# A hybrid attention and delta-rule layer on one core: masks behind the first level's sums, one more block of side work in the levels, and the attention merge behind the last level

## The reference, cut to what matters

```
kk = einsum('nbhid,nbhjd->nbhij', kc * bc, kc)
lower = where(tri_strict, kk * decay, 0) + eye(c)
sol = triangular_solve(lower, concat([vc * bc, kc * bc * exp(gcum)]))
attn = einsum('nbhid,nbhjd->nbhij', qc, kc) * decay
def step(s, xs):                     # one chunk after the other
    u = u0 - wk @ s
    o = qd @ s + attn @ u
    s = s * g_last + kd^T @ u
...
w = softmax(stack(lses), axis=0)     # merge of the three attention groups
o_att = sum(w[..., None] * stack(outs), axis=0)
```

## Time and profile before

| | |
|---|---|
| median of 3 runs | 1901.26 us (1900.22 to 1904.27) |
| the profiled execution | 1900.11 us, of it the span 1898.3 us |
| mean granted TensorE clock | 0.975 |
| TensorE busy in the span | 1793.2 us (94%) |
| VectorE, ScalarE, GpSimd busy | 45%, 28%, 21% |

### The profile page before, as it was taken

The page is one execution under the profiler, slowest core; times in us unless marked ns, Lnnn a source line. Parts: engine busy times, 40 slices in busy tenths (PEclk is TensorE's granted clock), DMA queues, the critical chain, the costliest instruction groups (busy, mean ns, idle before and its releaser), DMA issues.

```text
span 1898.3 us, 36967 instructions
## 1 busy us (share of the span) xinstructions
PE 1793.2 (94%) x14992; PEld 1735.9 (91%) x14992; DVE 845.2 (45%) x1548; ACT 533.9 (28%) x1048; POOL 393.4 (21%) x194
## 2 busy tenths in 40 slices
PE   7999999999978888999999779999999999999995
PEld 7999999999968787887999779999999999999994
DVE  3003346664545566645651444452144441144437
ACT  3223334444312333330221353331012221022211
POOL 2221111111111110111222342222222222222224
PEclk9999999999989999998999889999999999999997
DMA  4111112242522132314541113333333111111111
GB/s 169 44 44 43 42 64 76 80 179 82 214 86 90 61 108 72 97 46 169 200 160 45 45 67 116 128 120 117 116 117 127 44 44 45 45 47 53 41 62 78
DMA packets 68233, 170.13 MB, mean 90 GB/s; under 512 B 9448, under 2 KB 38280, under 8 KB 66832
## 3 DMA queue, kind: packets, MB, share of 16 engines
q1 hardware_dynamic: 67408, 167.68, 25.7%
q10 hardware_dynamic: 720, 0.92, 0.1%
HBM read 138.19 MB, written 57.79 MB: 103 GB/s over the span
## 4 chain that ended last, share of the span: by engine, by line
PE 85%; DVE 8%; issue 2%; DMA 2%; ACT 2%; POOL 1%; POOLq 0%; SPq 0%; DVEq 0%; ACTq 0%
PE U L720 60%; PE U L824 7%; PE U L1190 3%; PE B L720 2%; PE B L810 1%; PE B L785 1%; DMA stage<-in_wu 1%; PE B L802 1%; DVE stats L1973 1%; PE B L913 1%; PE B L987 1%; PE B L1138 1%; PE B L1015 1%; PE B L915 1%; DVE og L1683 1%
## 5 line engine op out<-in xcount | busy, mean ns | idle before, releaser
L638 POOL TENSOR_TENSOR wl<-stage,wh 128x1024 fp32r<-128x1024 f32 x127 | 310.3, 2444 | 1127.6 <-ACT wh L1211 1127.6
L720 PE MATMUL U<-xh,wh 128*128 128x344 f32 x1368 | 443.6, 324 | 0.2 <-ACT qkv L1215 0.2
L720 PE MATMUL U<-xl,wh 128*128 128x344 f32 x1368 | 437.1, 320 | 0.0
L720 PE MATMUL U<-xh,wl 128*128 128x344 f32 x1368 | 437.1, 319 | 0.0
L720 PE MATMUL U<-hh,wh 128*128 128x344 f32 x1056 | 338.8, 321 | 4.5 <-POOL hl L691 4.5
L720 PE MATMUL U<-hl,wh 128*128 128x344 f32 x1056 | 338.2, 320 | 0.0
L720 PE MATMUL U<-hh,wl 128*128 128x344 f32 x1056 | 337.4, 319 | 0.0
L720 PEld LDWEIGHTS U<-xh,wh 128*128 128x128 f32 x1368 | 257.3, 188 | 0.8 <-ACT qkv L1215 0.5
L720 PEld LDWEIGHTS U<-xh,wl 128*128 128x128 f32 x1368 | 257.2, 188 | 0.0
L720 PEld LDWEIGHTS U<-xl,wh 128*128 128x128 f32 x1368 | 257.1, 188 | 0.0
L720 PEld LDWEIGHTS U<-hh,wh 128*128 128x128 f32 x1056 | 199.3, 189 | 4.6 <-issue 4.6
(11 more groups left out here) (359 smaller groups left out, 2468.3 us busy)
## 6 DMA issues: line engine op xcount, KB each, us to landing
stage<-in_wu SPq DMA_DIRECT2D x126, 512.0 KB, 3.6
out_shift<-in_cache SPq DMA_DIRECT2D x16, 1022.0 KB
gate_scr<-gth SPq DMA_DIRECT2D x16, 516.0 KB, 3.0
gates<-gate_scr SPq DMA_DIRECT2D x8, 1032.0 KB, 5.0
dn_scr<-thb SPq DMA_DIRECT2D x12, 512.0 KB, 2.6
qkv<-in_xT SPq DMA_DIRECT2D x4, 1032.0 KB, 10.5
kvc<-in_cache SPq DMA_DIRECT2D x4, 1024.0 KB, 8.4
dqk<-dn_scr SPq DMA_DIRECT2D x8, 512.0 KB, 3.9
```

The source lines that it names most:

```text
L638: nc.gpsimd.tensor_tensor(wl[:, par, :], stage[:, par, :], wh[:, par, :].bitcast(F32), ALU.subtract).then_inc(w_lo, 1)
L720: ins = nc.tensor.matmul(dst, a[:, par, w], b[:, xk, third(j)], start=first and n == 0 and m == 0, stop=last and n == len(ks) - 1 and m == 2)
```

## The change

Four moves, all inside the tile loop; no instruction is added or taken away.

1. `FILLS[1]`: the quarters of the six levels go from (1, 0, 1, 0, 0, 2) to (1, 1, 2, 1, 1, 2). What `beside.rest()` has left behind level 5 goes from 7 quarters to 3.
2. `masks` is cut: `Loff` and `ATm` go to `late_masks`, which VectorE runs behind both additions of level 0, with `out_low(i - 2)` and the `amx` maxima behind it. The level 1 quarter stands before `state_read`, which waits for `ATm`.
3. VectorE's merge of the attention groups goes from levels 2 and 3 behind `out_norms(i - 1)`.
4. TensorE's turn of `ao` goes from level 5 behind `beside.rest()`, and ScalarE's `oh` copy behind its own `rest()`.

```diff
-FILLS = {1: (0, 2, 4, 1, (1, 0, 1, 0, 0, 2), 2), ...
+FILLS = {1: (0, 2, 4, 1, (1, 1, 2, 1, 1, 2), 2), ...
@@ TensorE, inside `for lv in range(LEVELS)`, behind y
                     if i > 0 and lv in (1, 3, 4):
+                        if lv == 1:
+                            beside.run(f_level[lv])
                         (state_read, updates, outputs)[lv // 2 if lv < 4 else 2](i - 1)
                     if lv == 5:
-                        pe.wait_ge(ao_ready, i + 1)
-                        pe.wait_ge(s_ready, i + 1)
-                        for n in range(2):
-                            ins = nc.tensor.transpose(B34[:, 0, n * P:(n + 1) * P], ao[:].rearrange(
-                                "p h e -> p (h e)")[:, n * P:(n + 1) * P], ident)
-                        ins.then_inc(ao_done, 1)
-                    beside.run(f_level[lv] + (2 if i == 0 and lv in (1, 3, 4) else 0))
+                        beside.run(f_level[lv])
+                    if lv not in (1, 5) or i == 0 and lv == 1:
+                        beside.run(f_level[lv] + (2 if i == 0 and lv in (1, 3, 4) else 0))
...
                 beside.rest()
+                pe.wait_ge(ao_ready, i + 1)
+                pe.wait_ge(s_ready, i + 1)
+                for n in range(2):
+                    ins = nc.tensor.transpose(B34[:, 0, n * P:(n + 1) * P], ...
+                ins.then_inc(ao_done, 1)
@@ VectorE, in masks
+            def late_masks(t):
                 nc.vector.scalar_tensor_tensor(Loff[LO], LT4[LO, :, HB:P], -1.0, Ew[LO, :, HB:P], ALU.mult, ALU.mult)
                 nc.vector.tensor_tensor(heads4(ATm[:, t % 2]), AT4, Ew[:], ALU.mult).then_inc(side_ready, 1)
@@ VectorE, behind the additions of level 0
                     if lv == 0:
+                        late_masks(i)
+                        if i > 1:
+                            out_low(i - 2)
+                        (the three amx maxima)
                         query_norms(i)
@@ VectorE, behind the levels
                     out_norms(i - 1)
+                dve.wait_ge(ae_exp, i + 1)
+                (abuf times weights, two additions, reciprocal, ao)
                 dve.wait_ge(ao_high, i + 2)
```

More of the change, by code:

```diff
@@ L402, in tiles @@
                 u += n
-        FILLS = {1: (0, 2, 4, 1, (1, 0, 1, 0, 0, 2), 2), 2: (2, 4, 6, 2, (2, 1, 2, 1, 1, 3), 4)}
+        FILLS = {1: (0, 2, 4, 1, (1, 1, 2, 1, 1, 2), 2), 2: (2, 4, 6, 2, (2, 1, 2, 1, 1, 3), 4)}
         def window(t):
@@ L1030, in _ @@
                 beside.rest()
+                pe.wait_ge(ao_ready, i + 1)
+                pe.wait_ge(s_ready, i + 1)
+                for n in range(2):
+                    ins = nc.tensor.transpose(B34[:, 0, n * P:(n + 1) * P], ao[:].rearrange(
+                        "p h e -> p (h e)")[:, n * P:(n + 1) * P], ident)
+                ins.then_inc(ao_done, 1)
             beside = Beside(U_BRANCH - BESIDE_SAMPLES, (U_BRANCH - BESIDE_SAMPLES) % 2, BESIDE_SAMPLES, quarter, start_unit)
@@ L1425, in _ @@
                     out_squares(i - 1)
+                beside.rest()
                 act.wait_ge(ao_done, i + 1)
@@ L1428, in _ @@
                     "p (n k) -> p n k", n=2), ACT.Copy).then_inc(ao_high, 1)
-                beside.rest()
             beside = Beside(U_BRANCH - BESIDE_SAMPLES, (U_BRANCH - BESIDE_SAMPLES) % 2, BESIDE_SAMPLES, quarter, start_unit)
@@ L1818, in _ @@
                 masks(i)
-                if i > 1:
-                    out_low(i - 2)
                 for lv in range(LEVELS):
@@ L1825, in _ @@
                         dn.link(nc.vector.tensor_tensor(Lb[lv % 2][:], LTq[:], lev(lv + 2), ALU.mult))
[L1827 to L1832, removed]
                     if lv < LEVELS - 1:
@@ L1852, in _ @@
                     if lv == 0:
+                        late_masks(i)
+                        if i > 1:
+                            out_low(i - 2)
+                        dve.wait_ge(att_in, i * 16 + 16)
+                        dn.link(nc.vector.tensor_tensor(amx[:, 0, :], abuf[:, 0, :, 65], abuf[:, 1, :, 65], ALU.max))
+                        dn.link(nc.vector.tensor_tensor(amx[:, 0, :], amx[:, 0, :], abuf[:, 2, :, 65], ALU.max))
+                        nc.vector.tensor_tensor(amx[:, 1:4, :], abuf[:, :, :, 65], amx[:, 0, :].unsqueeze(1)
+                                                .to_broadcast([P, 3, 4]), ALU.subtract).then_inc(ae_ready, 1)
                         query_norms(i)
@@ L1856, in _ @@
                     if lv == 2:
[L1857 to L1861, removed]
                         if i + 1 < TILES:
@@ L1866, in _ @@
                             decayed_state(i - 1)
[L1867 to L1871, removed]
                     if lv == 4 and i > 0:
@@ L1875, in _ @@
                     out_norms(i - 1)
+                dve.wait_ge(ae_exp, i + 1)
+                w3 = amx[:, 1:4, :].unsqueeze(3).to_broadcast([P, 3, 4, 65])
+                dn.link(nc.vector.tensor_tensor(abuf[:, :, :, 0:65], abuf[:, :, :, 0:65], w3, ALU.mult))
+                dn.link(nc.vector.tensor_tensor(abuf[:, 0, :, 0:65], abuf[:, 0, :, 0:65], abuf[:, 1, :, 0:65],
+                                                ALU.add))
+                dn.link(nc.vector.tensor_tensor(abuf[:, 0, :, 0:65], abuf[:, 0, :, 0:65], abuf[:, 2, :, 0:65],
+                                                ALU.add))
+                dn.link(nc.vector.reciprocal(amx[:, 4, :], abuf[:, 0, :, 64]))
+                nc.vector.tensor_tensor(ao[:], abuf[:, 0, :, 0:64], amx[:, 4, :].unsqueeze(2).to_broadcast(
+                    [P, 4, 64]), ALU.mult).then_inc(ao_ready, 1)
                 dve.wait_ge(ao_high, i + 2)
```

## The result

The changed kernel takes 1910.06 us (median of 20 runs, 1901.33 to 1916.72), the kernel before beside it 1901.51 us: ratio 1.0045, 95% interval 1.003 to 1.006. It is slower, by 8.6 us; forecast were 10.7 us, 1912 us.

The account below looks back on a forecast made before the run. TensorE, busy 94% of the span, was taken to bound the kernel. Profiled 1900.1 us + 10.7 structure + 0.1 clock = 1910.9, at the median's level 1912.1: forecast 1912 us, range 1903.5 to 1918 us.

Parts of the forecast that it names:

- Level 0: Start of a tile: with late masks, the wait for the addition to `X` shrinks from 1.66 to 0.22 us, -1.44 us.
- Level 5: y(5) to zt(5): without the turn of `ao` and its wait, 3.02 us becomes 2.04 us, -0.98 us.
- The quarters in the levels: Levels 1 to 4: three lone quarters at 0.83 us and a second in level 2 at 0.60, +3.09 us per tile.
- my model tile: Tile 4, 32.51 us at clock 1.00, the undisturbed tile whose timeline the per-tile terms were worked out from.
- From y(0) to zt(5): Levels 0 to 5 of a tile: 3.09 - 1.44 - 0.98 = +0.67 us, over tiles 1 to 7 +4.7 us.
- The tile's end: Behind zt(5): TensorE stops 1.9 and 1.2 us, K K at 9.28 instead of 8.51 us, +0.77 us; together +6.0 us.
- Structure: Whole kernel without the clock: 4.7 us from the levels + 6.0 us from the ends = +10.7 us.
- the low bound 4.6: Low end of the structure term: 0.57 us less per tile for quarters, 0.3 us less per end, +4.6 us.
- the sign of being wrong: Tiles shorter than 32.5 us at full clock would mean quarters fill unseen waits or the merge ends before three quarters.
- Clock: TensorE's clock: four falls behind level 0 go, -4.9 us; five come at tile ends, +5.0 us; sum about nothing.
- rival 3: Tile ends: every end falls at full price, 10.7 - 4.9 + 7 x 1.23 = +14.4, 1916 us; chance 0.16.
- Rival 1: Clock falls neither in level 0 nor at the end: +5.8, 1907 us, by low quarter costs 1903; chance 0.22.

Follow-up runs that it names:

- the two last runs: A quarter added in level 3: to the changed kernel with six left and old output scaled first, 1886.60 us; to late masks with level 5's quarters first, 1882.52 us.
- the kept-busy end: Changed kernel with idle matmuls in its two stops at the tile's end, 10 ahead of the turn of `ao`, 6 ahead of L901: 1902.74 us.

## Why the prediction was right, point by point

*Level 0* was forecast at -1.44 us; 3.62 became 2.15 us, -1.47. `state_read` did not wait for `ATm` (759.80, behind y(1) and the quarter). But this holds for tiles 2 to 7: in tile 1 level 0 took only 2.58 us before, so that 1.0 us of the gain that I counted seven times was not there.

*Level 5*, forecast -0.98 us: 3.02 became 2.06 us.

*The quarters in the levels* were over-sized: "+3.09 us". Level 1 (4.14 against 3.31) and level 2 (2.79 against 2.15) came as forecast. Level 4 was 3.86 against 3.16, +0.70, and level 3, forecast at 0.83, took 2.98 us where tile 4 of before took 2.97, tile 6 2.48 and tile 7, with no pause in that level, 2.42. Two things were wrong there. A lone quarter right behind y costs 0.83 us (level 1), but one behind the 128-wide products of levels 3 and 4 costs 0.56 and 0.70 us. And tile 4, my model tile, has a pause in level 3 (0.42 us, inside L1015) that belongs to no engine and that I took for a part of the level, so "the levels have no wait left" did not hold for it. In tiles 3 to 7 of the changed kernel no such pause stands in level 3; in tiles 1 and 2 there is one, of 1.16 and 1.62 us. The experiments with a quarter there agree (level 3 takes 2.97 to 3.16 us in tiles 5 to 7 of the two last runs, but for one of 3.71 us; without the quarter 2.42 to 3.73 us); why the pause goes was not tested.

From y(0) to zt(5) the forecast was +0.67 us per tile. Measured at full clock it is 17.97 us against 17.83 us in tile 6 and 18.23 us in tile 4: +0.14 or -0.26 us.

*The tile's end*: L901 forecast at 6.55 us, measured 6.43; stops forecast "1.9 us" and "another 1.2 us or so", measured 1.69 and 1.10; K K forecast at 9.28 us, measured 9.06, so +0.55 instead of +0.77 us per end. For tile 7, 6.43 against 5.12 us, +1.3 where +1.4 was forecast.

*Structure*: forecast 10.7 us, 5.7 us by the runs at equal clock, near the low bound 4.6. A tile at full clock, forecast near 33.9 us, took 32.64 us, closer to the sign of being wrong (under 32.5 us) than to the forecast. The traces add up to 3 to 6 us: 7 x 0.13 or 0.53 us (against tile 4 or 6), 1.0 us for tile 1, 0.8 us more at the end of tile 7, 0.2 us at that of tile 0.

*Clock*: forecast about 0 ("-4.9" and "+5.0"), measured +3.7 us. Both of its parts were too small. The four falls behind level 0 had cost 1.58, 1.40, 1.23 and 1.58 us, 5.8 us in place of 4.9, and all four are gone. The falls at the ends cost 1.59, 1.59, 1.62, 2.28 and 1.30 us in tiles 1, 2, 3, 4 and 6 of the profiled execution, 8.4 us in place of "five of 1.0", and a sixth stands behind tile 7; this execution is a long one, so the mean is less. The sum of +3.7 us is what rival 3 has for the clock (-4.9 and +8.6).

So the total of 8.6 us came nearer than its two terms: the structure was about half of its forecast, the clock that of a rival, and the two errors, 5 us down and 3.7 us up, cancelled in the main. That is luck; what was right by understanding is level 0, level 5, and the two stops with their lengths. That both stops weigh on the clock was right in kind, as the kept-busy end shows. That some tiles would fall twice was not foreseen: the falls inside tiles 1 and 2 stand right behind the pauses of 1.16 and 1.62 us. Rival 1, that the clock would fall nowhere, is out.

## What to carry to other kernels

When work is moved off an engine's busy stretch to a "free" one, count what covered that stretch, and whether the same change takes the cover away: here late masks were a gain, the quarters and the merge's move each nothing by itself, and the same move of the merge cost 22 us once masks and quarters had been moved. On a queue that is served in order, put the link that the next stage waits for ahead of the one that only a later stage needs; moving one VectorE instruction ahead of another was worth 14 us here. And price a stop of TensorE twice, once for its length and once for the slow clock that may follow; before the model tile is used as one, look in it for pauses that no engine explains.

## What the runs showed of the hardware that I had not expected

Runs of one kernel differ by 8 to 21 us, and this spread follows the time at TensorE's lower clock (0.4 us per us, with 0.6 to 2.4 us left over). In the tiles of the changed kernel a stop of 1.1 us, behind another of 1.7 us and 0.9 us of turns, decided over most of that time: without the second stop the time at the lower level fell from 102 to 79 us, with the first left as it was; without the first and with the second, no end of tiles 1 to 6 fell either.

TensorE also pauses where the profile names no engine: 5.0 us in all between 600 and 834 us before, 3.3 us in the changed kernel, 10.7 us with late masks alone, at places that move with the order of instructions. In the changed kernel the clock fell right behind the two longest, 1.16 and 1.62 us, in the kernel before behind one of 1.70 us and not behind one of 1.24 us. What they wait for no run here shows.
